# Folding a norm weight into the input weights, splitting rows straight from PSUM, and running the first two chunks third by third in a decoder mixer layer

## What is computed

```python
def mixer_inputs(h, pre, wi, w_up, b_gate, bf):
    (gq, gk, gv, glr, gg, pv, pg, fq, fk, fv, ff, fg) = jnp.split(rmsnorm(h, pre) @ wi, SPLIT_IDX, axis=-1)
    ...
    g = (jax.nn.log_sigmoid((glr @ w_up + b_gate).astype(f32)) / GLA_GATE_NORM)
    ...
    logf = jax.nn.log_sigmoid((ff + bf).astype(f32))
# rmsnorm(x, g): x * rsqrt(mean(x * x) + EPS) * g
```

## Time and profile before

| | us |
|---|---|
| median of 3 runs | 754.33 |
| lowest and highest | 752.61, 757.26 |
| profiled execution | 751.11 |
| its span, first to last instruction | 749.5 |
| TensorE busy | 703.8 |
| VectorE busy | 394.9 |
| ScalarE busy | 249.4 |
| GpSimd busy | 160.8 |

### The profile page before, as it was taken

How to read it: one execution, slowest core, us unless ns; L and a number is a source line. 1 busy time by engine, 2 the same in 40 slices (tenths; PEclk the granted TensorE clock), 3 DMA queues, 4 the chain that set the end, 5 groups by cost and what they waited for, 6 DMA issues and landing times.

```text
span 749.5 us, 12866 instructions
## 1 busy us (share of the span) xinstructions
PE 703.8 (94%) x4976; PEld 552.2 (74%) x4976; DVE 394.9 (53%) x691; ACT 249.4 (33%) x421; POOL 160.8 (21%) x176
## 2 busy tenths in 40 slices
PE   3699999999999999999999998999998999999995
PEld 2467999998888888999999954454655333588884
DVE  4921662525233321118999965345535798465343
ACT  6645442213011136322112033444542275312211
POOL 3481311311111110212121153313320000222120
PEclk9986999999999999999999999999999999999998
DMA  8211203131111012431210277847670240022332
GB/s 250 54 44 35 57 3 67 29 86 29 30 29 30 2 20 62 141 108 47 56 48 10 91 235 239 270 138 224 187 232 2 84 183 1 1 71 85 113 113 84
DMA packets 60725, 67.25 MB, mean 90 GB/s; under 512 B 15172, under 2 KB 50875, under 8 KB 60665
## 3 DMA queue, kind: packets, MB, share of 16 engines
q1 hardware_dynamic: 55497, 51.35, 23.0%
q0 software_dynamic: 5168, 15.08, 6.5%
HBM read 57.70 MB, written 8.68 MB: 89 GB/s over the span
## 4 chain that ended last, share of the span: by engine, by line
PE 82%; DVE 8%; ACT 4%; issue 3%; DMA 1%; SPq 0%; DVEq 0%; ACTq 0%
PE PS L1628 15%; PE PS L1629 14%; PE PS L1630 14%; PE PS L1593 4%; PE PS L1592 4%; PE PS L1594 4%; PE PS L1876 3%; PE PS L1893 3%; PE PS L1855 3%; PE PS L1916 2%; PE PS L1807 2%; DVE rec L1544 2%; PE PS L1820 1%; PE PS L1725 1%; DVE acc L528 1%
## 5 line engine op out<-in xcount | busy, mean ns | idle before, releaser
L1628 PE MATMUL PS<-xh,wh 128*128 128x368 f32 (+1 forms) x624 | 221.2, 354 | 0.4 <-POOL xl L538 0.4
L1629 PE MATMUL PS<-xl,wh 128*128 128x368 f32 (+1 forms) x624 | 208.9, 335 | 0.0
L1630 PE MATMUL PS<-xh,wl 128*128 128x368 f32 (+1 forms) x624 | 208.5, 334 | 0.0
L764 POOL TENSOR_TENSOR wl<-wr,wh 128x1024 fp32r<-128x1024 f32 (+1 forms) x26 | 63.7, 2451 | 296.5 <-ACT wh L900 296.5
L1628 PEld LDWEIGHTS PS<-xh,wh 128*128 128x128 f32 (+1 forms) x624 | 117.2, 188 | 12.7 <-issue 6.2
L1629 PEld LDWEIGHTS PS<-xl,wh 128*128 128x128 f32 (+1 forms) x624 | 117.6, 188 | 3.0
L1630 PEld LDWEIGHTS PS<-xh,wl 128*128 128x128 f32 (+1 forms) x624 | 117.5, 188 | 1.5
L1475 DVE CUSTOM_DVE_ANT_0 junk<-PS,RA 128x272 bf16<-128x272 f32 (+9 forms) x84 | 39.2, 507 | 41.1 <-PE PS L1880 29.0
L1338 DVE RECIPROCAL RA<-RA 128x1104 f32<-128x1104 f32 x8 | 56.4, 7053 | 0.3
L1592 PE MATMUL PS<-woh,yh 128*128 128x512 f32 (+1 forms) x144 | 56.3, 391 | 0.0
L1594 PE MATMUL PS<-woh,yl 128*128 128x512 f32 (+1 forms) x144 | 56.1, 389 | 0.0
(11 more groups left out here) (293 smaller groups left out, 1018.8 us busy)
## 6 DMA issues: line engine op xcount, KB each, us to landing
wr<-in_w_in_dram SPq DMA_DIRECT2D x24, 512.0 KB, 3.9
kpage<-in_cache_fox_k_dram SPq DMA_DIRECT2D x64, 192.0 KB, 3.9
pagesB<-in_cache_fox_v_dram POOLq DMA_DIRECT2D x32, 192.0 KB, 3.6
RA<-in_cache_fox_v_dram POOLq DMA_DIRECT2D x32, 192.0 KB, 4.0
YF<-in_x_prompt_dram SPq DMA_DIRECT2D x8, 512.0 KB, 6.4
xres<-in_x_prompt_dram SPq DMA_DIRECT2D x8, 512.0 KB, 3.8
out_y_p_dram<-zout SPq DMA_DIRECT2D x16, 256.0 KB, 2.0
wo_raw_a<-in_w_out_dram SPq DMA_DIRECT2D x6, 512.0 KB, 4.5
```

What stands on the lines that cost most here:

```text
L764: g.tensor_tensor(wl[:, c % 2, :, 0:m], wr[:, c % 2, :, 0:m], wh[:, c % 2, :, 0:m].bitcast(F32), ALU.subtract).then_inc(wlo_done, 1)
L1628: pe.matmul(out, high, xh[:, k, cols], start=(k == 0), stop=False)
L1629: pe.matmul(out, high, xl[:, k, cols], start=False, stop=False)
L1630: ins = pe.matmul(out, low, xh[:, k, cols], start=False, stop=(k == KT - 1))
```

## The change

Chunk 0's columns move together (22 of 32), and nine things are edited:

1. `gpre` isn't multiplied to x any more (`x_pre` and `xg` go) but to the weights: `w_scale(c)` on VectorE, for every chunk, in place in `wr`, at the head of VectorE's iteration c - 1; `w_high(c)` waits for it.
2. x_high and x_low read PSUM, by halves of four blocks; x_low is all on VectorE. One pair of banks (6 and 7) serves all tiles; transposes of a half wait for the low part of that half of the tile before.
3. Roots are made for two tiles at a time, and a Sqrt of a constant comes first on ScalarE.
4. w_low of chunks 0 and 1 is on VectorE; chunk 1's weights are loaded behind the fourth prompt tile.
5. `first_chunks`: chunks 0 and 1 run third by third, with the last four transposes between.
6. Chunk 0's low part lies in columns 32 to 63 of `wh`, so a block costs two products: both parts times xh (64 columns), high part times xl (32).
7. The gate product: `low_h` and `low_l` are split from PSUM (ScalarE, VectorE), w_up is split too, three fp32r products from 64 partitions; logf comes out of the same product, in rows 64 to 69 by a selecting block behind w_up.
8. Gates are side jobs of chunk 2 (`SIDE[1]`, steps 2 to 12), logf_rows and page_prefix the first jobs of chunk 5 (`SIDE[4]`), and every `extra` of the gate chain comes one chunk later.
9. GpSimd has no x_low and no w_low(1); `w_high(2)` stands ahead of `store(0)`.

```diff
-    s[0] = [("gate", g, t) for g in range(2) for t in range(3)]
-    s[3] = [("logf_rows",), ("page_prefix",)]
+    s[1] = [("gate", g, t) for g in range(2) for t in range(3)]
...
-    s[4] = [("v_rows", b) for b in range(10)] + [("hist",), ("pool_last", 0)]
+    s[4] = [("logf_rows",), ("page_prefix",)] + [("v_rows", b) for b in range(10)] + [("hist",), ("pool_last", 0)]
...
+        def x_halves(i):
+
+            t = XORDER[i]
+            for half in range(2):
+                ks = slice(4 * half, 4 * half + 4)
+                src = PS[:, 6 + half, :].rearrange("p (k t) -> p k t", t=P)
+                yield 2 * i + half + 1, [(src[:, :, r0:r1], (slice(0, P), ks, slice(col, col + r1 - r0)))
+                                         for r0, r1, col in xcols(t)]
...
             def w_high(c):
                 if c >= NCHUNK:
                     return
-                act.wait_ge(d_w[c % 2], W_COUNT[c])
+                act.wait_ge(wg_done, c + 1)
...
             act.wait_ge(wz, 1)
-            for i, t in enumerate(XORDER):
-                x_squares(t)
-                if i >= 2:
+            link(act.activation(zstat[:, 0:1], eps[:, :], ACT.Sqrt))
+            x_squares(0)
+            x_roots(0, 1)
+            for i in range(1, 9, 2):
+                x_squares(i)
+                if i >= 3:
                     x_high(i - 2)
...
+                x_squares(i + 1)
+                x_roots(i, 2)
+                x_high(i - 1)
+                if i == 3:
                     w_high(0)
+                    w_high(1)
             x_high(7)
             x_high(8)
-            w_high(1)
...
                 if c == C_LF:
                     act.wait_ge(in_full, c + 1)
-                    act.activation(thirds(glr), src[0:LR], ACT.Copy)
-                    act.activation(thirds(logf), src[32:32 + H], ACT.Copy).then_inc(done, 1)
+                    act.activation(thirds(low_h[0:64, :]), src[0:64], ACT.Copy).then_inc(low_high, 1)
...
+            def x_low(i):
+                for n_, parts in x_halves(i):
+                    dve.wait_ge(xhi_done, n_)
+                    for src, at in parts:
+                        ins = dve.tensor_tensor(xl[at], src, xh[at].bitcast(F32), ALU.subtract)
+                    ins.then_inc(xlo_done, 1)
+
+            def w_scale(c):
+
+                if c >= NCHUNK:
+                    return
+                dve.wait_ge(d_w[c % 2], W_COUNT[c])
+                if not c:
+                    dve.wait_ge(d_gpre, 16)
+                m = chunk_width(c)
+                w = wr[:, c % 2, :, 0:m]
+                dve.tensor_tensor(w, w, gpre[:, :, None].to_broadcast([P, KT, m]), ALU.mult).then_inc(wg_done, 1)
+
             x_scale(0)
             for i in range(9):
                 if i + 1 < 9:
                     x_scale(i + 1)
-                x_pre(i)
-                if i - 1 in DVE_LOW or i == 8:
-                    x_low(dve, i if i == 8 else i - 1).then_inc(xlo_dve, 1)
+                x_low(i)
+                if i == 1:
+                    w_scale(0)
+                    w_scale(1)
+                if i == 3:
+                    w_low(dve, 0)
+                    w_low(dve, 1)
...
             for c in range(1, NCHUNK + 1):
+                w_scale(c + 1)
                 store(c - 1)
...
+            def low_rank(t):
+
+                cols = slice(TH * t, TH * t + TH)
                 for k in range(KT):
+                    both = (PS[0:64, t, 0:TH], wh[:, 0, k, 0:64], xh[:, k, cols])
+                    rest = (PS[0:32, t, 0:TH], wh[:, 0, k, 0:32], xl[:, k, cols])
...
+            def first_chunks():
+
+                rows_at = {(0, 4): 6, (1, 3): 8}
+                pe.wait_ge(wlo_done, 2)
+                pe.wait_ge(whi_done, 2)
+                for t in range(3):
+                    x_low_done(pe, (3, 6, 8)[t])
+                    low_rank(t)
+                    if t < 2:
+                        x_transposes(5 + 2 * t)
+                    cols = slice(TH * t, TH * t + TH)
+                    for k in range(KT):
+                        high, low = wh[:, 1, k, :], wl[:, 1, k, :]
...
+                        if (t, k) in rows_at:
+                            x_transposes(rows_at[t, k])
+                ins.then_inc(in_full, 1)
...
-                    m = P if g == 0 else 64
-                    ins = pe.matmul(out[0:m, 0:TH], w_up[:, P * g:P * g + m], glr[:, TH * t:TH * t + TH],
-                                    start=True, stop=True)
+                        pe.wait_ge(wup_low, 1)
+                    m = P if g == 0 else 64 + H
+                    cols = slice(TH * t, TH * t + TH)
+                    for n_, (w, x) in enumerate(((wuh, low_h), (wuh, low_l), (wul, low_h))):
+                        ins = pe.matmul(out[0:m, 0:TH], w[0:64, P * g:P * g + m], x[0:64, cols], start=(n_ == 0), stop=(n_ == 2))
```

More of the change, by code:

```diff
@@ L455, in chunk_width @@
         def chunk_width(c):
-            return max(at + n for _, at, n in CHUNKS[c])
+            return 32 if c == C_LF else P
         def chunk_psum(c):
@@ L532, in cache_page, with w_low @@
             return cache[bass.ds(page, 1)].rearrange("a p n -> (a p) n")
[L534 to L540, removed]
-        XORDER = [NTILE] + list(range(NTILE))
-        DVE_LOW = (4, 6, 8)
-        def x_low_done(eng, i):
[L547 to L550, removed]
+        XORDER = [NTILE] + list(range(NTILE))
+        def x_halves(i):
[5 more added lines that the diff above has]
+                                         for r0, r1, col in xcols(t)]
+        def x_low_done(eng, i):
+            eng.wait_ge(xlo_done, 2 * (i + 1))
+        def w_low(eng, c):
+            eng.wait_ge(whi_done, c + 1)
+            if c >= 2:
+                eng.wait_ge(in_full, c - 1)
+            m = chunk_width(c)
+            low = wh[:, 0, :, 32:64] if c == C_LF else wl[:, c % 2, :, 0:m]
+            eng.tensor_tensor(low, wr[:, c % 2, :, 0:m], wh[:, c % 2, :, 0:m].bitcast(F32),
+                              ALU.subtract).then_inc(wlo_done, 1)
         block = ctx.enter_context(nc.Block())
@@ L756, in _ @@
                 keep(m[:, :], [[-1, P]], 0, 1, 1.0, ALU.not_equal, last=m is identb)
[L758 to L768, removed]
-                    x_low(g, i).then_inc(xlo_done, 1)
-                if i == 2:
-                    w_low(0)
-            g.wait_ge(xt_full, 9)
+            g.wait_ge(xt_full, 2 * 9)
             link(g.memset(reset, 1.0))
@@ L823, in _ @@
             for c in range(3, NCHUNK):
-                w_low(c)
+                w_low(g, c)
             g.wait_ge(in_full, NCHUNK)
@@ L1063, in _ @@
             for c in range(1, NCHUNK + 1):
+                if c == 1:
+                    w_high(c + 1)
                 store(c - 1)
-                w_high(c + 1)
+                if c > 1:
+                    w_high(c + 1)
                 for key in SIDE[c - 1]:
@@ new lines, in low_rank @@
+            def low_rank(t):
+                cols = slice(TH * t, TH * t + TH)
+                for k in range(KT):
+                    both = (PS[0:64, t, 0:TH], wh[:, 0, k, 0:64], xh[:, k, cols])
+                    rest = (PS[0:32, t, 0:TH], wh[:, 0, k, 0:32], xl[:, k, cols])
+                    if k:
+                        pe.matmul(*rest, start=False, stop=False)
+                    ins = pe.matmul(*both, start=(k == 0), stop=(k == KT - 1))
+                    if k == 0:
+                        pe.matmul(*rest, start=False, stop=False)
+                if t == 2:
+                    ins.then_inc(in_full, 1)
@@ new lines, in first_chunks @@
+            def first_chunks():
+                rows_at = {(0, 4): 6, (1, 3): 8}
+                pe.wait_ge(wlo_done, 2)
+                pe.wait_ge(whi_done, 2)
+                for t in range(3):
+                    x_low_done(pe, (3, 6, 8)[t])
[5 more added lines that the diff above has]
+                        high, low = wh[:, 1, k, :], wl[:, 1, k, :]
+                        out = PS[:, 3 + t, 0:TH]
+                        pe.matmul(out, high, xh[:, k, cols], start=(k == 0), stop=False)
+                        pe.matmul(out, high, xl[:, k, cols], start=False, stop=False)
+                        ins = pe.matmul(out, low, xh[:, k, cols], start=False, stop=(k == KT - 1))
+                        if (t, k) in rows_at:
+                            x_transposes(rows_at[t, k])
+                ins.then_inc(in_full, 1)
@@ L1633, in project_in @@
                         step = KT * t + k + 1
-                        if c == 0 and step in (2, 5, 8):
-                            x_transposes(6 + (step - 2) // 3)
                         upto = len(jobs) * (min(max(step, first), last) - first) // (last - first)
```

160 lines of the change are left out of this document (91 added, 69 removed).

## The result

| us | before | after |
|---|---|---|
| median of the timed runs | 753.47 (4 runs) | 759.82 (4 runs) |
| lowest and highest | 744.39, 757.26 | 754.04, 764.07 |
| profiled execution, its span | 751.11, 749.5 | 754.04, 752.3 |

The ratio is 1.0124, with a 95% interval of 1.0066 to 1.0182: slower by 1.2%, which is small and clear of 1. The forecast was 752.3 and faster than before. The profiled pair differs by only 2.9 us; that the medians differ by 6 to 10 is the second thing to explain.

What follows compares the result with a forecast made beforehand. TensorE, with 82% of the span, was taken to bound the kernel. About 5.0 us gained up to chunk 8 less 3.0 in the gating gave 2.0: 749.1 us profiled, median 752.3, range 743 to 759.

Steps and rivals of the forecast that it cites:

- The gates: Chunk 1 before held some 9 us of fallen clock; six split gates, now in chunk 2, cost 0.5 each, 3.0 us.
- the sum to P(8): End of chunk 8: start gain 22.7, less gates 3.0, idle 11.5 and clock 3.4; about 5 us earlier.
- New wait 1: Start of chunk 2: TensorE waits for w_low(2) behind GpSimd's constants, idle 3.1 us.
- the clock behind the waits: Half clock behind two idle times, ahead of chunk 2 and behind page_prefix: 3.4 us lost, bounds 0 and 6.
- The start: Chunks 0 and 1: transposes begin at 8.7, one table load; chunk 1 ends, P(1), at 50.5 against 73.2 us.
- New waits 2 to 4: Gate chain, one chunk later: TensorE idles 2.8 ahead of chunk 5, 4.1 at page_prefix, 1.5 at v_rows(0).
- The gating: Chunks 17 to 24: GpSimd goes first, VectorE takes 13.7 in chunks 18 to 21; row maximum 4.5 late, cost 3.
- A: Gating: VectorE's add goes first in all chunks, w_scale is hidden and the 3 us stay: 749.3; chance 0.25.
- B: Gating: GpSimd goes first in chunks 22 and 23 too, loss 9.3 for 3: slower, 759.6; chance 0.08.
- C: Gates of chunk 2: the clock falls again as at 52.3, 5 us lost: 757.3; chance 0.10.
- D: New waits are smaller than summed, no clock dips: 8 us more gained, 744; chance 0.15.
- E: Start isn't shortened as told, a tile takes 3.5 for 2.7 us: 3 us lost, 755; chance 0.07.

Runs made afterwards that it cites:

- b1: The kernel before, unchanged, profiled once more: chunk 2 starts at 65.1 us and the first row maximum comes at 427.4 us.
- second set: The changed kernel again, unchanged, beside 19 runs of the kernel before: medians 758.89 against 749.29 us, ratio 1.019.
- e0: The changed kernel once more, unchanged: median 758.89 us of 4 runs, profiled span 755.6 us.
- e4: Changed kernel with w_scale behind the gating's add, w_scale(5), w_scale(6) ahead of the gate chain, page_prefix behind v_rows, w_low(2) on VectorE, store(3) on ScalarE: 738.26 us, 0.9892.
- e1: Changed kernel with w_scale between the add and the reciprocal in the gating of chunks 17 to 24: median 755.94 us of 10, ratio 1.0082 to the kernel before.
- e6: e4 with each gate as one FP32 product from 64 partitions, splits made but not read: 739.88 us of 4, 0.987 to the kernel before.
- e7: e4 once more, unchanged, beside e6: 737.83 us of 4 against 746.43 for the kernel before, 0.987.

## Why the prediction was wrong

**Two steps failed. The first, and the one behind the credit, is in "The gates": "so some 9 us are the fallen clock", and with it P(1) at 73.2.** I took them for gained. In three of five profiles of the kernel before they aren't there: chunk 1 takes 18.3 in b1 (46.8 to 65.1) and 26.0 in the first profile, so the fall is 7.7 where it comes, and without it the start gains 65.2 - 50.2 = 15.0 for the 22.7 of my sum. By that sum the 2.0 gained turn into 6 lost. The three times that I had (752.61 to 757.26) didn't show it; later sets of 19, 7 and 7 runs have medians of 749.3, 746.2 and 746.4.

**The second is the sum to P(8), in three terms: the gates (5.4 for 3.0), the first wait (4.6 for 3.1) and the clock behind the waits (5.4 for 3.4).** This is what the profiled pair shows, where the base is the very execution that I read.

**The start was right.** Chunk 1 was done at 50.2 (50.5), one table load, the transposes from 8.1.

**The gates in chunk 2 were at their upper bound.** In the rows above, from 60.19 to 61.43 are 1.24 us for what takes 2 x 0.167 without a gate: 0.9 a gate and 5.4 for six, for 0.5 and 3.0. Three products are 0.5 of it; the other 0.4 are four distances of 0.26 to 0.28, where products go from one kind to another, for 0.167 at a stretch. I had the bound of 0.9 and chose 0.5 by the wrong row, products that follow others of their own kind. By the same count the FP32 gate of before takes 1.0 at full clock (18.3 less 12.1 for the 72 products, by six), where I had 0.82.

**New wait 1** was 4.6 for 3.1: from the first memset to w_low(2) GpSimd takes 10.9 for 9.0.

```profile
41.57 1.02 POOL L773 MEMSET YF<- 128x1104 f32 x1 [37.17 <-PE PS L1654]
...
52.42 2.33 POOL L559 TENSOR_TENSOR wl<-wr,wh 128x1024 fp32r<-128x1024 f32 x1
```

**New waits 2 to 4** were right in place and size: 2.9, 3.7 and 0.8 for 2.8, 4.1 and 1.5.

**The clock behind them** cost 1.7 and 3.7, together 5.4 for 3.4, at the two places that I had counted; the 2.94 ahead of chunk 5 had none behind it, as counted. P(8) came 1.2 earlier, not 5. The terms above leave some 0.3 of the gain; most of the rest is a wait of 0.69 that the kernel before has at 151.65, ahead of a pool product, and the changed one hasn't.

**The gating was right.** GpSimd went first in chunks 18 to 21 (13.7 an iteration, the add 2.9), VectorE in 22 to 24 (11.4), TensorE waited 1.6 for w_low(24) (1.3), and with P(8) 1.2 earlier as it came, 439.9 becomes 438.7, measured 438.45. GpSimd led by 0.07 us (380.17 against 380.24), in chunk 22 VectorE by 0.04, and both held in each of the two profiles. Only what the stage behind gives back was 0.3 and not 1.5; I had no row for the 1.5.

Together: 3.8 us at P(8) and 1.2 behind make 749.1 into 754.1 for the profiled execution, measured 754.04. The medians differ by more than this pair's 2.9, and in the second set the 9.6 split up as 2.9 + 4.9 + 1.8: the changed kernel's median lies 4.9 over its profiled execution (5.8 in the first set, where I had added 3.2), and the base's lies 1.8 under the execution I read. Most of it is thus in the changed kernel's other executions. Their clock was lower: 0.974 in the mean of all eight for 0.984 in the profiled one. e0's profile shows 3.3 us of it, behind the first row maximum; the rest has no trace.

**The rivals.** A fell (the add waits). B fell in its mechanism: VectorE was first in chunks 22 and 23. Its sign and its 759.6 came true all the same, for other reasons, which is luck. C fell, the clock stayed whole through the split gates. D and E fell too. The missing rival was that the half clock, and so the gain, isn't in every execution of the kernel before.

The Trainium skill, "TensorE: Matmul & The Clock Gate", "Why this matters for your kernels", puts a fall of the clock down to idle gaps. The rows behind 54.8 and 108.8 agree; those of the kernel before from 52.3 on, where the same instructions run once at 0.51 and once at 1.00 without an idle time right ahead, don't follow from it. Nor does the length of the idle time alone decide in these runs: half clock came behind 2.48 (near 575) and 2.67, and not behind 2.94.

## What to carry to other kernels

A half clock in one profile is an execution, not yet the kernel: to credit a gain to it takes more profiles than one, or more timed runs than three (19 of them went down to 743.5 against a profiled 751.1). A step that is added to every iteration belongs where the GpSimd work that it releases meets an instruction that it doesn't lengthen, here the reciprocal: w_scale cost 1.6 us a chunk ahead of the product and nothing behind the add. And when work is put into a queue behind a long chain, list everything behind that chain that another engine needs (here w_scale, then the PSUM copy), since removing one wait uncovers the next.

## What the runs showed of the hardware

- Same kernel, same instructions, whole or half clock: 52.3 to 60 us at 0.51 or at 1.00 (0.51 and 0.59 in two profiles, 1.00 in three). The idle time of 2.48 us near 575 us (555 to 570 in some) was met by half clock in every profile of this study, for 3.4 us in some (the changed kernel's first profile), 6.8 in e4, about 10 in e0 and 13.6 in others (b1, e1).
- Idle times of 4.6 and 3.7 us ahead of TensorE's work were followed by half clock, of 3.7 us and 7.6 us; one of 2.94 wasn't.
- One execution of e1 in ten had a mean granted clock of 0.566 and took 1100.65 us; it has no trace.
- Three fp32r products of 368 columns between others cost 0.9 us, 0.17 each and four changes of kind at 0.1 more; one FP32 product in their place costs 0.1 us more (chunk 2 in 18.0 us in e6 for 17.3 in e7).
- VectorE's add of one operand (0.72 alone) takes 2.92 when it comes 0.07 us behind the start of GpSimd's subtraction; when it comes 0.04 ahead, the subtraction takes 2.90 for 2.40. A scan takes 4.55 for 2.46 beside it, while the reciprocal (7.05) and the subtraction beside it (2.41) don't lengthen each other. The Trainium skill, "SBUF — State Buffer", "SBUF: two separate sides", has a port pair that these two engines share and that one holds for its whole instruction; the add and the scan agree with it, and by the rows the reciprocal doesn't take it.
